# A diffusion block on one core: first piece of the output projection prepared in attention's last body, last modulation sums ahead of the key split

## What is computed

```python
m_lat = adaln(c, w_mod[l], b_mod[l])
h = modulate(rms_norm(ys, norm_mix[l]), m_lat[0], m_lat[1])
q, k, v, u = mixer_proj(h, w_in[l])
att = neighbourhood_attention(q, k, v, cache_k[:, l], cache_v[:, l], rpb[l])
mix = jnp.concatenate([att, pool_mixer(u, w_pool[l], pool_scale[l])], axis=-1) @ w_out[l]
ys = ys + m_lat[2][:, None] * mix
...
```

## Time and profile before

| what | us |
|---|---|
| median of 3 runs | 3995.26 |
| lowest, highest | 3994.15, 3995.73 |
| the profiled execution, its own time | 3987.93 |
| its span from first to last instruction | 3985.9 |
| TensorE busy | 3759.7 (94%) |
| VectorE busy | 2459.9 (62%) |
| ScalarE busy | 1775.5 (45%) |
| GpSimd busy | 476.3 (12%) |

### The profile page before, as it was taken

One profiled execution on the slowest core, in us unless ns is written; L12 is line 12 of the kernel. 1 busy time (PEld: TensorE's weight loads), 2 busy tenths in 40 slices (PEclk: granted clock), 3 DMA queues, 4 the chain that ended last, 5 costly groups with the idle time before them and its releaser, 6 DMA issues. The chain is left out here.

```text
span 3985.9 us, 63531 instructions
## 1 busy us (share of the span) xinstructions
PE 3759.7 (94%) x22936; PEld 3256.6 (82%) x22936; DVE 2459.9 (62%) x4637; ACT 1775.5 (45%) x2654; POOL 476.3 (12%) x517
## 2 busy tenths in 40 slices
PE   8899999999799999899997799999999999999992
PEld 4688888888698888788886788888888888999881
DVE  5755555555566666332324777777777777777774
ACT  3611111111277776311104566666666666666553
POOL 0000000000264644010100000000000000000000
PEclk9999999999999999899998799999999999999996
DMA  9434434433564644635416588878887878878886
GB/s 377 149 125 137 137 124 137 137 132 129 170 183 146 198 143 146 261 134 214 151 52 260 196 264 260 265 257 265 269 259 258 263 265 257 275 260 264 263 252 249
DMA packets 556499, 825.31 MB, mean 207 GB/s; under 512 B 24288, under 2 KB 426112, under 8 KB 544640
## 3 DMA queue, kind: packets, MB, share of 16 engines
q1 hardware_dynamic: 532352, 702.27, 53.2%
q0 software_dynamic: 24064, 121.93, 9.3%
HBM read 717.18 MB, written 108.00 MB: 207 GB/s over the span
## 5 line engine op out<-in xcount | busy, mean ns | idle before, releaser
L2079 DVE TENSOR_TENSOR e_wlo<-e_raw,e_whi 128x1024 fp32r<-128x1024 f32 x768 | 905.1, 1219 | 323.1 <-ACT e_whi L1998 320.1
L2216 PE MATMUL ps<-e_xs,e_whi 128*128 128x320 f32 x4096 | 1052.8, 344 | 7.7 <-DVE e_xs L2093 6.9
L2216 PE MATMUL ps<-e_xs,e_wlo 128*128 128x160 f32 x4096 | 934.8, 238 | 0.0
L1998 ACT ACTIVATE e_whi<-e_raw 128x1024 fp32r<-128x1024 f32 x768 | 766.3, 1049 | 283.9 <-DMA e_raw<-in_w_up 111.4
L2216 PEld LDWEIGHTS ps<-e_xs,e_wlo 128*128 128x128 f32 x4096 | 770.4, 191 | 0.7
L2216 PEld LDWEIGHTS ps<-e_xs,e_whi 128*128 128x128 f32 x4096 | 752.4, 188 | 10.3 <-issue 7.6
L2234 PE MATMUL ps<-e_whi,e_h 128*128 128x512 f32 x1024 | 403.4, 394 | 1.2 <-DVE e_h L2119 1.0
L481 DVE SCALAR_TENSOR_TENSOR p_acc<-p_modraw,cT,p_acc 128x256 f32<-128x256 f32 x960 | 396.9, 488 | 0.0
L531 PE MATMUL ps<-hhi,p_whi 128*128 128x512 f32 (+1 forms) x1536 | 383.9, 357 | 8.5 <-DVE p_wlo L463 8.5
L531 PE MATMUL ps<-hhi,p_wlo 128*128 128x512 f32 (+1 forms) x1536 | 380.5, 355 | 0.0
L531 PE MATMUL ps<-hlo,p_whi 128*128 128x512 f32 (+1 forms) x1536 | 380.5, 355 | 0.0
(11 more groups left out here) (252 smaller groups left out, 5345.6 us busy)
## 6 DMA issues: line engine op xcount, KB each, us to landing
e_raw<-in_w_gate SPq DMA_DIRECT2D x64, 2048.0 KB, 8.1
e_raw<-in_w_up SPq DMA_DIRECT2D x64, 2048.0 KB, 8.1
e_raw<-in_w_down SPq DMA_DIRECT2D x64, 2048.0 KB, 8.1
p_modraw<-in_w_mod SPq DMA_DIRECT2D x128, 512.0 KB, 3.5
m_raw<-in_w_mod SPq DMA_DIRECT2D x16, 2048.0 KB, 13.2
p_raw<-in_w_in SPq DMA_DIRECT2D x64, 512.0 KB, 4.7
o_raw<-in_w_out SPq DMA_DIRECT2D x16, 2048.0 KB, 9.2
projT<-p_out_st POOLq DMA_DIRECT2D x30, 640.0 KB, 3.7
```

The costliest lines, as they stand in the source:

```text
L1998: nc.scalar.activation(piece(whi, c, q), piece(raw, c, q), ACT.Copy).then_inc(w_hi_made, 1)
L2079: nc.vector.tensor_tensor(piece(wlo, c, q), piece(raw, c, q), piece(whi, c, q).bitcast(F32), ALU.subtract).then_inc(w_lo_made, 1)
L2216: last = nc.tensor.matmul(bank[:, 0:cols], w[:, s, at:at + P], xs[:, k, 0:cols], start=(k == 0 and w is whi), stop=(k == KD - 1 and w is whi))
```

## The change

Two things are changed.

**The order at the last quarter of the input projection.** VectorE's last two halves of `mod_sums` now stand ahead of the wait for `piece_used`, of `high_keys()` and of `low_queries()`.

**The start of the output projection.** `output_projection` has no block of its own any more; its programs are called from attention's. In the last body SyncE issues the load of the first half of weights and of the first quarter of rows between the pool loads and the seventh pool stores. ScalarE makes the four high pieces behind units 11 to 14, VectorE the four low pieces behind units 12 to 15. To have room, three of attention's tensors change places and all tensors of the projection lie at fixed addresses over those that are finished. Behind the last body SyncE loads quarter 1 of the rows, the second half of weights, and quarters 2 and 3. TensorE makes the 120 products of the first half at once, then the gate rows, then the second half. The gated sum is written back to PSUM instead of a tile of its own, and a bank counts as free once x is added (`y_ready`), not once the gate is applied (`gated`).

```diff
-        output_projection(nc, sem, locals())
+    out = output_projection(nc, sem, v)
+    att = attention(nc, sem, v, sums_read, RING + 2 * LASTC, out)
...
                     elif following:
                         make_lo(n + 1, 0)
-                    elif q == NQ - 1:
+                    for i in range(2):
+                        mod_sums(n, q, i)
+                    if q == NQ - 1 and not following:
                         dve.wait_ge(piece_used, quarters_used(2))
                         high_keys()
                         low_queries()
-                    for i in range(2):
-                        mod_sums(n, q, i)
...
+    WEIGHTS_AT = {11: 0, 12: 1, 13: 2, 14: 3}
...
                 store_pool(j - 1)
                 load_pool(j, j + 1)
+                sp.wait_ge(bias_made, 12 * J)
+                sp.wait_ge(k_lo_made, 2 * J)
+                first_weights()
+                sp.wait_ge(mean_stored, 32 * NPOOL + FIRST)
+                sp.wait_ge(att_stored, 32 * j + AHEAD)
+                sp.wait_ge(scored, j * U + W)
+                first_rows()
                 store_pool(j)
...
+                if last and u in WEIGHTS_AT:
+                    if WEIGHTS_AT[u] == 0:
+                        act.wait_ge(bias_made, 12 * J)
+                        act.wait_ge(batch_turned, J * NB)
+                    high_weights(0, 0, WEIGHTS_AT[u])
...
+                if last and u - 1 in WEIGHTS_AT:
+                    if WEIGHTS_AT[u - 1] == 0:
+                        dve.wait_ge(mean_stored, 32 * NPOOL + FIRST)
+                    low_weights(0, 0, WEIGHTS_AT[u - 1])
...
+        def make_hi(m, s, q):
+            act.wait_ge(w_loaded[s], (m + 1) * 16)
...
+        def projection():
+            load_mix(0, 1)
+            load_w(0, 1)
+            load_mix(0, 2)
+            load_mix(0, 3)
...
-                        pe.wait_ge(gated, at - BANKS + 1)
+                pe.wait_ge(y_ready, at - BANKS + 1)
...
             if m % NB == 0:
                 by_rows(m, 0)
+                if m == 0:
+                    turn_gates()
                 by_rows(m, 1)
```

More of the change, by code:

```diff
@@ L711, in sync @@
     def sync(sp):
+        first_weights, first_rows, projection = out.sync(sp)
         def load_head(j, h):
@@ L802, in following @@
                 sp.wait_ge(s, n)
+            projection()
         return first_loads, following
@@ L900, in following @@
             pool.wait_ge(mean_stored, 32 * NPOOL + FIRST)
+            pool.wait_ge(att_stored, 32 * J + AHEAD)
+            pool.wait_ge(pooled_stored, 32 * NPOOL + AHEAD)
+            out.gpsimd(pool)
         return low_keys, biases, following
     def scalar(act):
+        high_weights, projection = out.scalar(act)
         def scale_q(j, h):
@@ L1041, in following_bodies @@
             body(J - 1, True, True)
+            act.wait_ge(out_lo, J * W + AHEAD)
+            projection()
         return scaled_queries, value_blocks, following_bodies
     def vector(dve):
+        low_weights, projection = out.vector(dve)
         def stats(j, u):
@@ new lines, in gpsimd, with load_x @@
+    def gpsimd(pool):
+        def load_x(m, t):
+            at = m * TPG + t
+            if at >= 2:
+                pool.wait_ge(x_in[at % 2], at // 2 * 16)
+            pool.dma_start(xy[t][:], tile_of(xcat, m, t)).then_inc(x_in[at % 2], 16)
+        for t in range(TPG):
+            load_x(0, t)
+        for m in range(2 * NB):
+            for t in range(TPG):
+                at = m * TPG + t
+                pool.wait_ge(y_ready, at + 1)
+                pool.dma_start(tile_of(y_d, m, t), xy[t][:]).then_inc(y_stored, 16)
+                pool.wait_ge(y_stored, (at + 1) * 16)
+                if m < 2 * NB - 1:
+                    load_x(m + 1, t)
@@ new lines, in scalar, with projection @@
+    def scalar(act):
+        def make_hi(m, s, q):
+            act.wait_ge(w_loaded[s], (m + 1) * 16)
+            if m and s and q == NP - 1:
+                act.wait_ge(tile_done, m * TPG)
+            elif m:
+                act.wait_ge(piece_used, (m - 1) * PIECES + s * NP + q + 1)
+            nc.scalar.activation(whi[s][:, q * QP:(q + 1) * QP], raw[s][:, q * QP:(q + 1) * QP], ACT.Copy
+                                 ).then_inc(w_hi_made, 1)
+        def projection():
+            for m in range(2 * NB):
+                for s in range(2):
+                    if m or s:
+                        for q in range(NP):
+                            make_hi(m, s, q)
+        return make_hi, projection
@@ L1490, in router @@
+    return Programs(sync, gpsimd, scalar, vector, tensor)
 def router(nc, sem, v):
```

340 lines of the change are left out of this document (162 added, 178 removed).

## The result

The changed kernel takes 3999.84 us (median of 20 runs) where the kernel before takes 3994.87 beside it (20 runs): ratio 1.0014, 95% interval 1.0008 to 1.0021. It is slower by 5 us; 18 us less was predicted, and 3977 is far outside what was measured. The profiled execution took 4000.25 us, with a span of 3998.3.

The account below looks back on a forecast made before the run. TensorE was taken as full inside the stages, with waits of 16.51 and 24.46 us at attention's two edges. Terms -15 + 11 - 14 = -18 took 3995.3 to 3977 us, range 3969 to 3988.

Parts of the forecast that it names:

- The sum: Whole kernel: -15 at attention's front edge, +11 in its last body, -14 at the projection's start, together -18 us.
- Part 1: Front edge of attention: modulation sums ahead of the key split start attention earlier, gain 15 us, bounds 12 and 17.
- Part 2a: Last body of attention: ScalarE waits for the projection's first weights, landing at 1614; loss 11 us, bounds 7.5 and 22.
- the 1619 of equal shares: Last body, rival 1: rows and weights share the queues, weights land late; loss 16 to 22 us; chance 0.17.
- Part 2b: Start of the output projection: first products straight behind the last attention matmul; gain 14 us, bounds 11 and 17.
- Rival 4: Last body: ScalarE's wait for the weights outweighs all gains, kernel slower, about 4003 us; chance 0.02.
- The three terms that were given a size: Front edge of attention -15 us, last body +11, start of the output projection -14.
- the two put at nothing: Loss given back in attention's first body, and a changed pitch of the projection's 1920 products: each predicted 0 us.

Follow-up runs that it names:

- e6: Changed kernel with the output projection's weights and rows mlo all at multiples of 256 bytes: 3986.07 us, ratio 0.9980, 0.2267 us a product.
- e7: Changed kernel with projection weights and rows mlo at multiples of 256 bytes, first weights' four splits behind units 15 to 18: 3975.03 us, ratio 0.9951.
- e8: Kernel before with modulation sums first and GpSimd reordered: second head's low keys ahead of first window means, next biases after first pair's split: 3979.47 us, ratio 0.9961.
- e3: Changed kernel with the output projection's weights moved to multiples of 256 bytes, rows mlo left 128 bytes behind one: ratio 1.0010, 0.2311 us a product.

## Why the prediction was wrong

**The missing term, the first step that failed.** The sum took the 1920 products over unchanged, 0.228 us each, and asked only whether sums in PSUM and later banks would slow them; the answer there (nothing) was right, and the question too narrow. "All tensors of the projection lie at fixed addresses" stands in the change, and I counted no price for it. It is 12.8 us: e4, the kernel before with 128 unused bytes, is 12.75 us slower, and e6, the changed kernel with its tiles moved back, 13.6 us faster. This alone turns a gain of 6 into a loss.

**Part 1 held at the edge and not behind it.** 15 us was right (15.1). The second step that failed is that GpSimd's next chain starts 6 us earlier and has 5.95 us to spare, so that the second head's low keys come 12 us earlier and TensorE doesn't notice. The chain did start 6.7 us earlier, but waited 6.68 us for its loads (4.72 before), and the low keys began only 9.8 us earlier, when the units were 13 to 18 us ahead. They ended at 1103.7, and TensorE waited 1.57 us for them, with late units behind. Then the phase of the engines had moved by 6 to 15 us, and a split of finished pairs fell into the low keys and biases: 7.31 us instead of 0.35, with ScalarE idle 6.29 and TensorE 4.72. Of 15.1 us 6.6 were left. Since e7 loses nearly as much without a held split, how the loss divides between the late keys and the split stays open. Nothing in the front edge's rows shows this, but the trace of before had the same thing once, in body 6 (6.30 us for one such split), and I did not look for rows that take twenty times their median. The Trainium skill, page SBUF — State Buffer, section Who interferes with whom, says that a VectorE instruction with two inputs in SBUF contends with a GpSimd instruction that reads SBUF; of VectorE's two-port modes it says that whoever issues first gets the shared pair for the whole instruction. The trace agrees that the two collide (0.5 to 1.2 us for a split inside the biases instead of 0.29), but here the loser could wait for several instructions of GpSimd, not one: 10.24 us in e8 over four of 1.1 and six of about 1 us each.

**Part 2a was right in kind and near in size.** I had the landing at 1614; it is 1607.94 in a trace that is 6.6 us ahead there, 1614.5 in the clock of before, 10.9 us behind the issue at 1597.08, with 2.6 MB of rows issued right behind. That is the time worked out from the queue's order, and not the 1619 of equal shares. With the rule of the Trainium skill, page DMA: Bandwidth & Descriptors, section Queues, rings and completion order, the trace agrees. The restart to the next scores took 6.3 us, not 5.8 (granted clock 0.50 from 1609 to 1616, 0.77 in the 6 us behind), and what follows costs 2.6 us instead of 1. In all 13.6 for 11, inside its bounds of 7.5 to 22. The upper bound doesn't follow from its parts: a landing at 1622.7 gives 19.7, and with the splits in series 26.7.

**Part 2b was right.** 12.8 for 14; the wait for the second rows is 5.5 us, not 3.3. Their first load is issued at 1645.06, 8.4 us behind the end of attention and not 6.2, since it stands behind the landing of the last stores; by the row named there (1.4 and 5.46) it would have been 6.8. The 2.4 us lost by the first 14 products are 2.6 by their row.

**Rival 4**, the slower one, asked for a landing 36 us after the issue. The sign came from elsewhere: no rival held a cost spread over all products. The three terms that were given a size came near it (15.1, 13.6 and 12.8 for 15, 11 and 14); the two put at nothing, 8.5 and 12.8 us, outweigh the gain.

## What to carry to other kernels

Moving tiles is a change of its own. Before it, note for every long run of matmuls how the two operands' start addresses stand to each other modulo 256 bytes, and look at the pitch afterwards; one unused tile of 128 bytes cost 13 us here, and 9 in another stage. The better distance was not the same in the two stages, so it has to be measured. A gain at an edge shifts the phase of everything behind it: search the trace of before for operations that take many times their median, since each may be a collision that the shift can move, double or remove. A split that waits for a load goes where the load has landed, counted from its issue and the queue ahead, not where there is room on the engine.

## What was unexpected of the hardware

- The distance of two fp32r operands in SBUF, streamed less loaded, changes the pitch of 512-column products: 0.2267 us at 0 (mod 256 bytes), 0.2289 at 64, 0.2333 at 128 and 192, at the full granted clock. The rows loaded for the next product seem to count too (e3). In the input projection, with 256-column products among them, the order is the other way (195.0 ns a product at 128, 197.2 at 0).
- A VectorE subtraction of 128x128 that takes 0.29 us was held for 6.3 to 10.24 us when it fell among GpSimd's low keys with biases right behind: until the last bias or its end. Not every one is held so: in body 5 of the trace of before it fell in the same place (at 1461.90, biases from 1463.31) and took 1.67 us. When it falls inside the biases alone it takes 0.5 to 1.2 us.
